# One core, two transformer blocks: the first eight experts named early, a second selection spread between dot products, and the last output slab by token tiles

## The chip, the cores and the metric

The kernel runs on one core of a Trainium2 chip. Its time is the device time of one execution in microseconds (us); three timed runs of the kernel before gave 3590.76, 3593.22 and 3593.61, so the median is 3593.22 us. A core has TensorE (PE) for matrix products, VectorE (DVE), ScalarE (ACT), GpSimd (POOL), and SyncE (SP), which here only issues transfers. The sixteen DMA engines are shared by the queues of SP, ACT and POOL. Each engine works through its own list of instructions in order and waits on semaphores.

## What is computed

256 tokens of width 2048 pass through two blocks. The end of the first one is a layer of 16384 single-neuron experts, and the end of the second one is an output product with a layer norm:

```python
def peer(h, ...):                       # h: 256 x 2048, 8 heads
    q = (h @ w_query)                   # per head two halves of 128
    s1, s2 = q[..., 0] @ sub_keys_1.T, q[..., 1] @ sub_keys_2.T   # 128 scores each
    v1, i1 = top_k(s1, 16);  v2, i2 = top_k(s2, 16)
    cand = v1[:, None] + v2[None, :]    # 256 pairs
    top_s, pos = top_k(cand, 16)        # 16 pairs, position in the 16 x 16 square
    idx  = i1[pos // 16] * 128 + i2[pos % 16]
    gate = softmax(top_s)
    act  = (expert_down[idx] * h).sum(-1)            # 16 dots of 2048
    return sum_k gate * gelu(act) * expert_up[idx]   # 16 scaled rows of 2048
...
y = (o * silu(z)) @ w_out               # end of the second block, 2048 x 2048
x = layer_norm(alpha * x + y, g, b)     # the kernel's output
```

All of it is float32. The kernel makes a float32 product from three: an operand is split into a rounded high part and the rest (the low part), and high*high, low*high and high*low are added.

## The kernel before, in words

Weights come in parts of 256 rows by 512 columns (512 KB). SP loads a part into one of four ring places, ACT rounds it into the high part (`split_hi`, in the second block `mla_hi`), POOL or DVE subtracts it from the original to get the low part (`split_lo`, `mla_lo`), and PE multiplies: 12 products of 128x512 a part, six for each token tile of 128. Eight parts are a slab of 512 output columns. SP loads the next part into a ring place when its low part has been made (`lo_made`), and ACT overwrites a high part when PE has used it (`parts_used`).

**The expert layer** works in row heads: a row head is one token tile of one of the eight heads, so there are 16, in four rounds of four. Row head 0 is tile 0 of head 0, row head 1 is tile 0 of head 1, row heads 2 and 3 are the same two heads for tile 1.

1. `first_queries_pe`, `first_queries_act` and `first_queries_dve` make the queries of round 0 (the slab W_PQ). PE first does the eight parts for tile 0. ACT then scales them (`take_tile_rows`), PE turns them (`turn_tile_queries`), ACT copies them (`take_tile_queries`), PE scores them against the keys (`score_tile_keys`) and ACT copies the scores. Meanwhile PE does the eight parts for tile 1; the turn stands behind the first of these and the scoring behind the second. DVE scales the normed input for both tiles (`h2`).
2. DVE selects in `choose(chosen, step)`, steps 0 to 5: the best 16 of two lists (0 and 1), the best 16 of 256 pairs (2 and 3), the decoding of these into expert numbers (4 and 5). Before the change it does all of `choose(0)` (row head 0), which releases POOL by `experts_ready`, then all of `choose(1)`, then the 16 dots of row head 0.
3. POOL gathers one row of 2048 floats for each of 128 tokens with an indirect DMA (1 MB a row). The order is fixed by `row_table`: the 16 down rows of row head 0, then in turn an up row of head h and a down row of head h+1. There are eight places, four for down and four for up rows; row head 0's down rows use both. `load_row` waits until the row that had the place is used, and POOL issues in order. The first row also waits until PE has used all parts of W_PQ for both tiles, since held parts lie in the up places.
4. DVE multiplies a down row with `h2` and sums it (`dot_row`). After 16, ACT does the gelu (`gelu_head`), DVE multiplies by the gates (`weigh_head`), ACT spreads each weight on a diagonal (`spread_weight`), and PE adds the up rows with these (`sum_row`).
5. The weights of round 1's queries (slab W_PQ+1) are split meanwhile. POOL makes the low parts of parts 0 to 3 before it starts gathering. DVE makes those of parts 4 to 7 behind the dots 1, 3, 5 and 7 of row head 0. PE then makes the queries, ACT takes them and then rounds the first four parts of slab W_PQ+2. SP can load each of these four only when one of the low parts 4 to 7 is there. All of this stands in ACT's list ahead of the gelu of row head 0 (the end of `first_queries_act`, L1144 to L1154; the gelu is at L2127).

**The end of the kernel** is the product `mo` in four slabs of eight parts, part by part and in each part both tiles (`mla_part`). Behind the last part DVE adds the slab to the residual (L1755), takes the moments, ACT the root, DVE normalises four quarters of both tiles (`ln_last`), and SP stores a quarter of both tiles when it is done.

Of the kernel before, what the change touches and what calls it, by code (L numbers as in the profile page):

```python
# [7 lines left out]
F32 = mybir.dt.float32  # L8
# [3 lines left out]
ALU = mybir.AluOpType  # L12
# [10 lines left out]
PK = 2  # L23
# [253 lines left out]
M_FIRST = PARTS * W_CQ  # L277

# [79 lines left out]
def program(nc, I, out, table, stream, wide, narrow, latent, early, matrices):  # L358
    ctx = ExitStack()
    with ctx:  # L360
# [98 lines left out]
        gain_all = down_rows[:, ROWS - 1]  # L459
# [76 lines left out]
        ringf = ring.rearrange("p s k n -> p s (k n)")  # L536

# [46 lines left out]
        normal_high, tile_made = sem("normal_high"), sem("tile_made")  # L584

# [472 lines left out]
        def first_queries_pe(pe):  # L1058
# [62 lines left out]
        def first_queries_act(act):  # L1121
# [32 lines left out]
        def first_queries_dve(dve):  # L1154
# [19 lines left out]
            for t in range(NT):  # L1174
                m = nc.vector.scalar_tensor_tensor(out=h2[:, t], in0=X[:, t], scalar=full_inv[:, t:t + 1], in1=gain_all,
                                                   op0=ALU.mult, op1=ALU.mult)
            m.then_inc(h2_ready, 1)
# [212 lines left out]
        def mla_fill(sp):  # L1390

            at = {"uq": 0, "ckv": 0, "": 0}
            for n, (kind, _, _) in enumerate(M_ORDER):
                sp.wait_ge(lo_made, M_FIRST + n - RING + 1)
# [4 lines left out]
        def mla_hi(act, n):  # L1399

            act.wait_ge(part_in[n % RING], 16 * ((M_FIRST + n) // RING + 1))
            act.wait_ge(parts_used, M_FIRST + n - RING + 1)
            at = slice(0, mla_width(n))
            nc.scalar.activation(w_hif[:, n % RING, at], ringf[:, n % RING, at], ACT.Copy).then_inc(hi_made, 1)  # L1404
# [32 lines left out]
        def mla_part(pe, n):  # L1437
# [31 lines left out]
            by_tile = [(t, k) for t in range(NT) for k in range(PK)]  # L1469
            by_row = [(t, k) for k in range(PK) for t in range(NT)]  # L1470
            for step, (t, k) in enumerate(by_tile if (kind, i) == ("mo", 3) and last else by_row):
# [6 lines left out]
                    if (kind, i) == ("mo", 3) and last and step == PK - 1:  # L1478
                        mm.then_inc(tile_made, 1)
# [227 lines left out]
        def mla_dve(dve, n):  # L1707
# [40 lines left out]
            if kind == "mo" and u == PARTS - 1:  # L1748
                for t in range(NT):
                    if i == 3 and t == 0:  # L1750
                        dve.wait_ge(tile_made, 2)
                    else:
                        mla_made(dve, kind, i, u)
# [3 lines left out]
                    if i == 3:  # L1757
                        slab_moments(dve, i, [t])
                if i < 3:
                    slab_moments(dve, i)  # L1760
# [151 lines left out]
        def ln_last(dve):  # L1912

            dve.wait_ge(ln_in, 64)
            for q in range(4):
                at = slice(q * NC, (q + 1) * NC)
                for t in range(NT):
                    nc.vector.scalar_tensor_tensor(out=X[:, t, at], in0=X[:, t, at], scalar=ln_moments[:, t, 0:1],
                                                   in1=last_gain[:, at], op0=ALU.subtract, op1=ALU.mult)
                dve.drain()  # L1920
                for t in range(NT):
                    last = nc.vector.scalar_tensor_tensor(out=X[:, t, at], in0=X[:, t, at],
                                                          scalar=full_inv[:, t:t + 1], in1=last_shift[:, at],
                                                          op0=ALU.mult, op1=ALU.add)
                last.then_inc(ln_done, 1)
# [1280 lines left out]
```

## Time and profile before

| | |
|---|---|
| median of three runs | 3593.22 us |
| the profiled execution's own time | 3590.01 us |
| its span | 3588.2 us |
| PE busy | 3246.1 us (90%) |
| DVE, ACT, POOL busy | 1746.6, 1332.4, 2196.0 us |
| moved by DMA | 936.79 MB, mean 261 GB/s |
| of these gathered by POOL | 538.74 MB |
| mean granted clock of TensorE | 0.984 |

The span goes from the first to the last instruction of one traced execution. The page of the profile splits it into 40 slices of 89.7 us; the expert layer's gathers lie in slices 10 to 24, and in slices 11 to 23 (897 to 2063 us) the 16 DMA engines are busy nine tenths or more and move 417 to 421 GB/s. Outside of slices 10 to 24 the rate is 139 to 230 GB/s and PE is busy nine tenths of nearly every slice. A full clock is 1.0, which is 2.4 GHz, and 0.5 is 1.2 GHz.

### The profile page before, as it was taken

How to read it: one execution, taken by the hardware profiler on the slowest of the kernel's cores; microseconds unless marked ns; L12 is line 12 of the kernel's file. 1: busy time of each engine (PE TensorE's matmuls, PEld its weight loads, DVE VectorE, ACT ScalarE, POOL GpSimd, SP SyncE). 2: the span in 40 equal slices, each digit the busy share in tenths (PEclk: the TensorE clock that was granted, in tenths of full speed). 3: DMA queues.
4: the chain of work that ended last, by engine and by line, in shares of the span. 5: the costliest groups of instructions: out<-in, count | busy, mean ns of one | idle time of the engine just before them, and what ended most of it. 6: DMA issues, size and time to landing. Idle time of an engine off the chain costs nothing.

```text
span 3588.2 us, 38812 instructions
## 1 busy us (share of the span) xinstructions
PE 3246.1 (90%) x13642; PEld 2304.9 (64%) x13642; DVE 1746.6 (49%) x2565; ACT 1332.4 (37%) x2037; POOL 2196.0 (61%) x1221
## 2 busy tenths in 40 slices
PE   9999999996787788777777789999999999999998
PEld 7888878884343334322322348888888888878886
DVE  8998264238566457544744452222222223435443
ACT  6776575442111011000100014444444444445553
POOL 2021767876545545454555438888788778878666
PEclk9999999998999999999999999999999999999999
DMA  7455545659999999999999985555555545555444
GB/s 230 139 150 139 169 148 161 225 186 378 419 419 420 421 418 420 421 419 421 421 417 421 419 339 187 176 172 174 166 175 174 171 166 176 174 178 181 147 143 163
DMA packets 232701, 936.79 MB, mean 261 GB/s; under 512 B 28112, under 2 KB 31184, under 8 KB 165968
## 3 DMA queue, kind: packets, MB, share of 16 engines
q0 software_dynamic: 76288, 538.74, 36.3%
q1 hardware_dynamic: 152784, 391.96, 33.6%
q10 hardware_dynamic: 3456, 3.77, 0.3%
q8 instruction: 110, 1.80, 0.2%
q14 instruction: 63, 0.52, 0.0%
HBM read 927.04 MB, written 2.10 MB: 259 GB/s over the span
## 4 chain that ended last, share of the span: by engine, by line
PE 64%; DMA 25%; DVE 5%; POOL 2%; issue 1%; DVEq 1%; ACT 1%; ACTq 0%; SPq 0%
PE products L671 41%; DMA arena<-peer_up_in,arena 20%; PE products L2120 7%; PE products L1476 7%; DMA arena<-peer_down_in,arena 4%; POOL arena L2066 2%; DVE arena L2075 1%; PE products L1207 1%; PE products L2682 1%; PE products L1313 1%; PE products L2644 1%; PE products L1230 1%; POOL weights_low L1410 1%; DVE weights_low L630 0%; PE products L1450 0%
## 5 line engine op out<-in xcount | busy, mean ns | idle before, releaser
L630 POOL TENSOR_TENSOR weights_low<-arena,weights_high 128x1024 fp32r<-128x1024 f32 x484 | 1187.9, 2462 | 367.8 <-ACT weights_high L618 323.9
L2120 PE MATMUL products<-arena 128*128 128x512 f32 x1984 | 940.5, 621 | 288.4 <-DMA arena<-peer_up_in,arena 230.1
L618 ACT ACTIVATE weights_high<-arena 128x1024 fp32r<-128x1024 f32 x604 | 637.8, 1059 | 972.0 <-PE products L671 952.5
L671 PE MATMUL products<-weights_high,input_high 128*128 128x512 f32 x2416 | 984.7, 408 | 14.2 <-DVE weights_low L630 12.6
L671 PE MATMUL products<-weights_low,input_high 128*128 128x512 f32 x2416 | 945.7, 391 | 0.0
L671 PE MATMUL products<-weights_high,input_low 128*128 128x512 f32 x2416 | 943.3, 390 | 0.0
L2120 PEld LDWEIGHTS products<-arena 128*128 128x128 f32 x1984 | 372.0, 196 | 839.0 <-issue 427.2
L2075 DVE SCALAR_TENSOR_TENSOR arena<-arena 128x2048 f32<-128x2048 f32 x256 | 586.0, 2292 | 524.5 <-DMA arena<-peer_down_in,arena 524.0
L2066 POOL DMA_INDIRECT arena<-peer_up_in,arena x256 | 385.8, 1507 | 528.0 <-PE products L2120 504.3
L671 PEld LDWEIGHTS products<-weights_high,input_high 128*128 128x128 f32 x2416 | 455.4, 189 | 110.0 <-DVE weights_low L630 14.3
L671 PEld LDWEIGHTS products<-weights_low,input_high 128*128 128x128 f32 x2416 | 454.2, 188 | 98.8
L671 PEld LDWEIGHTS products<-weights_high,input_low 128*128 128x128 f32 x2416 | 455.6, 189 | 92.3 <-issue 4.5
L2066 POOL DMA_INDIRECT arena<-peer_down_in,arena x256 | 282.5, 1104 | 113.3 <-issue 75.3
L1410 POOL TENSOR_TENSOR weights_low<-arena,weights_high 128x1024 fp32r<-128x1024 f32 (+2 forms) x120 | 268.8, 2248 | 96.2 <-ACT weights_high L1404 93.4
L2136 ACT ACTIVATE arena<-arena 128x128 f32<-128x128 f32 x248 | 91.5, 397 | 561.5 <-PE products L2120 541.6
L1404 ACT ACTIVATE weights_high<-arena 128x1024 fp32r<-128x1024 f32 (+2 forms) x116 | 113.3, 977 | 143.9 <-PE products L1476 133.1
L1476 PE MATMUL products<-weights_high,arena_rounded 128*128 128x512 f32 (+1 forms) x512 | 155.4, 384 | 0.0
L630 DVE TENSOR_TENSOR weights_low<-arena,weights_high 128x1024 fp32r<-128x1024 f32 x120 | 146.2, 1222 | 9.7 <-ACT weights_high L618 8.8
L1247 DVE TENSOR_TENSOR arena<-products,arena 128x128 f32<-128x128 f32 x96 | 29.8, 352 | 239.9 <-PE products L1207 239.9
L2389 POOL COPY arena<-arena 128x252 f32<-128x252 f32 x16 | 19.8, 1266 | 206.7 <-DVE arena L2484 206.7
L1782 DVE TENSOR_TENSOR arena<-products,arena 128x1024 f32<-128x1024 f32 (+3 forms) x41 | 34.3, 838 | 188.1 <-PE products L671 185.1
L2127 ACT ACTIVATE arena<-arena 128x16 f32<-128x16 f32 x16 | 3.5, 217 | 286.8 <-DVE arena L2080 286.8
(352 smaller groups left out, 3038.0 us busy)
## 6 DMA issues: line engine op xcount, KB each, us to landing
arena<-dsa_in SPq DMA_DIRECT2D x320, 512.0 KB, 3.5
arena<-w_in_in SPq DMA_DIRECT2D x128, 512.0 KB, 3.8
arena<-mla_wide_in SPq DMA_DIRECT2D x88, 512.0 KB, 3.5
arena<-w_attn_o_in SPq DMA_DIRECT2D x32, 512.0 KB, 4.3
arena<-w_out_in SPq DMA_DIRECT2D x32, 512.0 KB, 4.7
arena<-peer_w_query_in SPq DMA_DIRECT2D x32, 512.0 KB, 7.8
arena<-dsa_w_out_in SPq DMA_DIRECT2D x32, 512.0 KB, 3.7
arena<-glu_w_b_in SPq DMA_DIRECT2D x16, 512.0 KB, 3.8
```

The costliest lines, as they stand in the source:

```text
L618: nc.scalar.activation(w_hi[:, u % RING, :, at], ring[:, u % RING, :, at], ACT.Copy).then_inc(hi_made, 1)
L630: ops.tensor_tensor(w_lo[:, u % RING, :, at], ring[:, u % RING, :, at], w_hi[:, u % RING, :, at].bitcast(F32), op=ALU.subtract).then_inc(l ...
L671: mm = nc.tensor.matmul(PS[:, bank(b) + t, 0:width], x[:, x0 + n, at], y, start=n == 0 and m == 0, stop=n == len(parts) * PK - 1 and m == 2)
L1207: mm = nc.tensor.matmul(PS[:, D_SCORE_BANK, at:at + seen], QKD[:, buf, k, 0, t * P:(t + 1) * P], QKD[:, buf, k, 1, 0:seen], start=True, st ...
L1230: nc.tensor.matmul(PS[:, O_BANK, col:col + SEQ], VD[:, buf, g, 0], PTD[:, s % 2, 0:2 * P], start=g == 0, stop=False)
L1404: nc.scalar.activation(w_hif[:, n % RING, at], ringf[:, n % RING, at], ACT.Copy).then_inc(hi_made, 1)
L1410: nc.gpsimd.tensor_tensor(w_lof[:, n % RING, at], ringf[:, n % RING, at], w_hif[:, n % RING, at].bitcast(F32), op=ALU.subtract).then_inc(l ...
L1476: mm = nc.tensor.matmul(banks[:, t, 0:width], x[:, x0 + PK * u + k, q], y, start=u == 0 and k == 0 and m == 0, stop=last and k == PK - 1 a ...
L2066: pool.indirect_dma_start(row_place(kind, h, n), None, I["peer_" + kind][0], bass.IndirectOffsetOnAxis(ap=experts[:, r, t, p, n:n + 1], ax ...
L2075: nc.vector.scalar_tensor_tensor(out=row, in0=row, scalar=1.0, in1=h2[:, t], op0=ALU.mult, op1=ALU.mult, accum_out=acts[:, h % 2, n:n + 1])\
L2120: mm = nc.tensor.matmul(PS[:, SUM_BANKS[q]], diag[:, d % ROWS], row[:, q * NC:(q + 1) * NC], start=h % 2 == 0 and n == 0, stop=bool(last))
L2136: nc.scalar.activation(diag[:, d % ROWS], ident, ACT.Copy, scale=weights[:, h % 2, n:n + 1]).then_inc(diag_ready, 1)
```

## The change

Three things change. First, in `choose(0)` the first eight experts are decoded directly behind the first eight maxima (`halve_best`, `name_experts`) and POOL is released for eight rows; the other eight follow. For this PE turns and scores tile 0 before it starts on tile 1, only one tile of `h2` is scaled ahead of the choice (the other behind the first dot of row head 1; the gain's vector waits in its place and is loaded later), and POOL makes three low parts ahead of the gathers and the fourth behind the fourth row. Second, the six steps of `choose(1)` stand behind the dots 0 to 5 of row head 0, and the low parts 4 to 7 of W_PQ+1 behind the dots 9, 11, 13 and 15. Third, the last slab of `mo` is done by tiles: its last four parts are rounded into the space of the normed input, so that all eight parts are there; PE does tile 0 with all of them, then tile 1; DVE finishes tile 0 while PE does tile 1; eight stores replace four. DVE makes the last five low parts in place of POOL.

```diff
@@ first_queries_pe
             mm.then_inc(queries_made, 1)
+            turn_tile_queries(pe, 0)
+            score_tile_keys(pe, 0)
             for u in range(PARTS):
                 query_part(pe, 0, u, [1])
-                if u == 0:
-                    turn_tile_queries(pe, 0)
-                if u == 1:
-                    score_tile_keys(pe, 0)
@@ first_queries_act
             take_tile_queries(act, 0)
-            next_hi(act, 0)
             take_tile_scores(act, 0)
             load_keys(act, 1)
-            for u in range(1, RING):
+            for u in range(RING):
                 next_hi(act, u)
@@ choose, with halve_best and name_experts cut out of its steps 3 to 5
+            best = slice(TOPK // 2, TOPK) if chosen == 0 else slice(0, TOPK)
+            if chosen == 0 and step == 2:
+                dve.drain()
+                for s in range(2):
+                    halve_best(dve, chosen, s, slice(0, TOPK // 2))
+                name_experts(dve, chosen, slice(0, TOPK // 2))
             if step in (4, 5):
...
+                halve_best(dve, chosen, step - 4, best)
             if step == 5:
...
+                name_experts(dve, chosen, best)
@@ POOL
-            split_lo(pool, nc.gpsimd, W_PQ + 1, 0, range(RING))
+            split_lo(pool, nc.gpsimd, W_PQ + 1, 0, range(RING - 1))
             pool.wait_ge(h2_ready, 1)
             pool.wait_ge(parts_used, PARTS * (W_PQ + 1))
             for kind, h, n in ROW_ORDER:
-                if kind == "down" and n == 0 and (h < 3 or h % 4 == 0):
-                    pool.wait_ge(experts_ready, h // 4 + 3 if h >= 4 else h + 1)
+                if kind == "down" and (h == 0 and n == TOPK // 2 or n == 0 and (h < 3 or h % 4 == 0)):
+                    pool.wait_ge(experts_ready, experts_of(h, n))
                 load_row(pool, kind, h, n)
+                if (kind, h, n) == ("down", 0, RING - 1):
+                    split_lo(pool, nc.gpsimd, W_PQ + 1, 0, [RING - 1])
...
-            for n in range(len(M_ORDER)):
+            for n in range(POOL_LAST):
                 mla_lo(pool, n)
@@ DVE
-            for chosen in range(2):
-                for step in range(CHOICES - 1):
-                    choose(dve, chosen, step)
+            for step in range(CHOICES - 1):
+                choose(dve, 0, step)
             for n in range(TOPK):
                 dot_row(dve, 0, n)
-                if n % 2 and n // 2 < RING:
+                if n < CHOICES - 1:
+                    choose(dve, 1, n)
+                if n % 2 and n // 2 >= RING:
                     dve.wait_ge(hi_made, PARTS * (W_PQ + 2))
-                    split_lo(dve, nc.vector, W_PQ + 1, 0, [RING + n // 2])
+                    split_lo(dve, nc.vector, W_PQ + 1, 0, [n // 2])
...
+                    if (h, n) == (0, 0):
+                        scale_rows(dve, 1)
                     rows_dve(dve, h, n)
...
-            for n in range(len(M_ORDER) + 1):
+            for n in range(M_LAST):
                 mla_dve(dve, n)
-            row_moments(dve)
-            ln_inverse(dve, 1)
-            ln_last(dve)
+            for n in range(POOL_LAST, M_LAST + PARTS):
+                last_lo(dve, n)
+            mla_dve(dve, M_LAST)
+            for t in range(NT):
+                last_rows(dve, t)
@@ the last slab: mla_hi rounds parts 4 to 7 without waiting for parts_used, into the space of XH and XL
+        def last_lo(dve, n):
+            dve.wait_ge(hi_made, M_FIRST + n + 1)
+            nc.vector.tensor_tensor(mla_half(1, n), ringf[:, n % RING], mla_half(0, n).bitcast(F32), op=ALU.subtract)\
+                .then_inc(last_low, 1)
+        def last_slab(pe):
+            for t in range(NT):
+                for u in range(PARTS):
...
+                    for k in range(PK):
+                        for m, (x, y) in enumerate(((YHR, hi), (YLR, hi), (YHR, lo))):
+                            mm = nc.tensor.matmul(banks[:, t], x[:, PK * u + k, q], y, ...)
+                mm.then_inc(last_made, 1)
+        def last_rows(dve, t):
+            dve.wait_ge(last_made, t + 1)
+            # residual, moments, root on ACT, four quarters of one tile, each released to SP
@@ SP
+            for t in range(NT):
+                for q in range(4):
+                    sp.wait_ge(ln_done, PARTS + 4 * t + q + 1)
+                    sp.dma_start(out[0, t * P:(t + 1) * P, at], X[:, t, at]).then_inc(out_done, 16)
```

## Rows read from the trace of the kernel before

**Rows 1.** Page, part 4: the chain that ended last, by line.

```profile
PE products L671 41%; DMA arena<-peer_up_in,arena 20%; PE products L2120 7%; PE products L1476 7%; DMA arena<-peer_down_in,arena 4%; POOL arena L2066 2%; DVE arena L2075 1%; PE products L1207 1%; PE products L2682 1%; PE products L1313 1%; PE products L2644 1%; PE products L1230 1%; POOL weights_low L1410 1%; DVE weights_low L630 0%; PE products L1450 0%
```

**Rows 2.** Windows: length, busy PE, PEld, DVE, ACT, POOL (instructions); clock, DMA, GB/s.

```profile
872.00:876.00 4.00, 4.00 (x6) 1.40 (x6) 2.22 (x2) 0.32 (x2) 3.39 (x3) 0.50 1.02 424
1100.00:1500.00 400.00, 317.57 (x740) 137.83 (x739) 228.38 (x306) 44.56 (x103) 196.46 (x155) 0.97 1.01 420
```

**Rows 3.** Chain of waits in order of time, its last long piece: start, length, what.

```profile
3516.31 53.08 PE products L1476 x234
```

**Rows 4.** Timeline of PE, 795 to 900 us: start, length, instruction [idle before <-releaser].

```profile
801.04 1.05 PE L1089 MATMUL products<-arena 128*128 128x128 f32 x8
...
871.59 16.56 PE L2120 MATMUL products<-arena 128*128 128x512 f32 x32 [14.39 <-ACT arena L2136]
```

**Rows 5.** Timeline of DVE, 802 to 832 us.

```profile
802.76 0.49 DVE L1955 MAX8 arena<-arena 128x8 f32<-128x128 f32 x2 [1.82 <-ACT arena L1118]
...
809.67 2.02 DVE L1999 TENSOR_SCALAR arena<-arena 128x16 uint32<-128x16 uint32 x1
...
815.50 0.18 DVE L2019 CAST arena<-arena 128x16 uint32<-128x16 f32 x1
...
826.40 2.29 DVE L2075 SCALAR_TENSOR_TENSOR arena<-arena 128x2048 f32<-128x2048 f32 x1
...
830.83 1.22 DVE L630 TENSOR_TENSOR weights_low<-arena,weights_high 128x1024 fp32r<-128x1024 f32 x1
```

**Rows 6.** Timeline of ACT, 798 to 870 us.

```profile
798.11 0.69 ACT L1106 ACTIVATE arena<-products,arena 128x512 f32<-128x512 f32 x1 [3.13 <-PE products L671]
...
810.34 0.69 ACT L1106 ACTIVATE arena<-products,arena 128x512 f32<-128x512 f32 x1 [4.25 <-PE products L671]
...
860.85 1.06 ACT L618 ACTIVATE weights_high<-arena 128x1024 fp32r<-128x1024 f32 x1 [2.58 <-DMA arena<-peer_w_query_in]
861.93 1.28 ACT L2127 ACT_TABLE_LOAD   x1
869.27 0.22 ACT L2127 ACTIVATE arena<-arena 128x16 f32<-128x16 f32 x1 [6.05 <-DVE arena L2080]
```

**Rows 7.** Timeline of POOL, 804 to 879 us.

```profile
804.27 7.38 POOL L630 TENSOR_TENSOR weights_low<-arena,weights_high 128x1024 fp32r<-128x1024 f32 x3 [0.34 <-ACT weights_high L1097]
816.60 1.05 POOL L2066 DMA_INDIRECT arena<-peer_down_in,arena  x1 [4.94 <-DVE arena L2019]
...
860.66 0.95 POOL L2066 DMA_INDIRECT arena<-peer_up_in,arena  x1 [8.91 <-DVE arena L2075]
...
878.12 1.89 POOL L2066 DMA_INDIRECT arena<-peer_up_in,arena  x1 [1.84 <-PE products L2120]
```

**Rows 8.** Line L2066, gathers issued at 821.73, 860.66 and 878.12 us, from issue.

```profile
DMA to landing us min/median/max: 11.5/11.5/11.5
...
DMA to landing us min/median/max: 8.8/8.8/8.8
...
DMA to landing us min/median/max: 12.2/12.2/12.2
```

**Rows 9.** Tile peer_w_query_in: weight parts issued 826 to 900 us, beside gathered rows.

```profile
DMA to landing us min/median/max: 10.3/10.9/11.9
```

**Rows 10.** Tile peer_w_query_in: weight parts issued 803 to 812 us, without gathers.

```profile
DMA to landing us min/median/max: 3.4/3.6/3.7
```

**Rows 11.** Timeline of DVE, 3571 us to the end.

```profile
3571.16 0.67 DVE L1755 SCALAR_TENSOR_TENSOR arena<-arena,products 128x512 f32<-128x512 f32 x1
...
3573.68 1.41 DVE L1918 SCALAR_TENSOR_TENSOR arena<-arena 128x512 f32<-128x512 f32 x2
...
3583.61 1.41 DVE L1922 SCALAR_TENSOR_TENSOR arena<-arena 128x512 f32<-128x512 f32 x2
```

**Rows 12.** Timeline of ACT at the start of the last slab; of SP at the end.

```profile
3549.07 1.06 ACT L1404 ACTIVATE weights_high<-arena 128x1024 fp32r<-128x1024 f32 x1 [1.66 <-PE products L1476]
...
3576.61 8.81 SPq L2897 DMA_DIRECT2D out<-arena  x4
```

More of the change, by code:

```diff
@@ L277 @@
 M_FIRST = PARTS * W_CQ
+M_LAST = len(M_ORDER) - PARTS
+POOL_LAST = M_LAST + RING - 1
 def mla_turns():
@@ L536, in program @@
         ringf = ring.rearrange("p s k n -> p s (k n)")
+        beside = [x[:].rearrange("p k t -> p (k t)").rearrange("p (s n) -> p s n", s=RING) for x in (XH, XL)]
         part_in = [sem(f"part_in{s}") for s in range(RING)]
@@ L1173, in first_queries_dve, with scale_rows @@
             dve.wait_ge(gain_in, 16)
[L1174 to L1177, printed above, removed]
+            scale_rows(dve, 0)
+        def scale_rows(dve, t):
+            nc.vector.scalar_tensor_tensor(out=h2[:, t], in0=X[:, t], scalar=full_inv[:, t:t + 1], in1=gain_all,
+                                           op0=ALU.mult, op1=ALU.mult).then_inc(h2_ready, 1)
         def hi_part(act, n):
@@ new lines, in mla_half @@
+        def mla_half(a, n):
+            return beside[a][:, n - M_LAST - RING] if n >= M_LAST + RING else (w_hif, w_lof)[a][:, n % RING]
+        def last_lo(dve, n):
[3 more added lines that the diff above has]
+        def last_slab(pe):
+            banks = mla_bank("mo", 3)
+            mla_emptied(pe, "mo", 3, 0)
+            for t in range(NT):
+                q = slice(t * P, (t + 1) * P)
+                for u in range(PARTS):
+                    n = M_LAST + u
+                    if t == 0:
+                        pe.wait_ge(lhs_lo, L_MO + u + 1)
+                        if n < POOL_LAST:
+                            pe.wait_ge(lo_made, M_FIRST + n + 1)
+                        else:
+                            pe.wait_ge(last_low, n - POOL_LAST + 1)
+                    for k in range(PK):
+                        hi, lo = (mla_half(a, n)[:, k * NC:(k + 1) * NC] for a in range(2))
+                        for m, (x, y) in enumerate(((YHR, hi), (YLR, hi), (YHR, lo))):
+                            mm = nc.tensor.matmul(banks[:, t], x[:, PK * u + k, q], y, start=u == 0 and k == 0 and m == 0,
+                                                  stop=u == PARTS - 1 and k == PK - 1 and m == 2)
+                mm.then_inc(last_made, 1)
@@ L1406, in mla_lo, with last_roots @@
+        def last_roots(act, t):
+            act.wait_ge(summed, 2 + t)
+            nc.scalar.activation(full_root[:, t:t + 1], ln_moments[:, t, 1:2], ACT.Sqrt, bias=eps_ln).then_inc(roots, 1)
         def mla_lo(pool, n):
@@ L1468, in mla_part @@
             last = u == (UP_PARTS if kind in ("uq", "ukv") else PARTS) - 1
-            by_tile = [(t, k) for t in range(NT) for k in range(PK)]
-            by_row = [(t, k) for k in range(PK) for t in range(NT)]
-            for step, (t, k) in enumerate(by_tile if (kind, i) == ("mo", 3) and last else by_row):
+            for k in range(PK):
+                for t in range(NT):
                     at = slice(k * width, (k + 1) * width)
@@ L1910, in finish_rows @@
                                                op0=ALU.mult, op1=op)
[L1912 to L1925, printed above, removed]
         def ln_load(sp, n):
@@ L2893, in _ @@
             ln_load(sp, 1)
[L2894 to L2898 removed]
+            for t in range(NT):
+                for q in range(4):
+                    at = slice(q * NC, (q + 1) * NC)
+                    sp.wait_ge(ln_done, PARTS + 4 * t + q + 1)
+                    sp.dma_start(out[0, t * P:(t + 1) * P, at], X[:, t, at]).then_inc(out_done, 16)
+            sp.wait_ge(out_done, 16 * 4 * NT)
         @block.gpsimd
@@ L3023, in _ @@
                 mla_act(act, n)
-            ln_act(act, 1)
+            for t in range(NT):
+                last_roots(act, t)
         @block.vector
@@ L3155, in _ @@
                 normal_turn_pe(pe, u)
-            for n in range(len(M_ORDER)):
+            for n in range(M_LAST):
                 mla_part(pe, n)
```

100 lines of the change are left out of this document (61 added, 39 removed).

## The prediction

> **What bounds the kernel.** I read the chain of waits first: 41% of the span is weight products, 20% and 4% are gathers of up and down rows on the way [rows 1]. The windows say which of the two rules where: between 1100 and 1500 us the DMA engines are never free (share 1.01, 420 GB/s) while PE is busy 318 of 400 us [rows 2]. So the expert layer is a stream of 1.05 MB rows at 2.5 us each; it ends earlier only if it starts earlier and never runs dry, and a hole in it is never made up. Behind it PE rules to the end: the last piece of the chain is 234 products in 53.08 us, 0.227 us each [rows 3], and then, from 3569.4, 18.8 us of the span remain for the layer norm and the stores. The change touches the start of the stream and these last microseconds. I work out each in the clock of the profiled execution.
>
> **A. The first gather.** POOL issues the first row at 816.60, having waited for DVE's choice, which ended at 815.68 [rows 5, 7]. Now:
>
> - *DVE starts earlier.* ACT has the rows of tile 0 at 798.80 [rows 6] and PE scores at 801.04 [rows 4]. In between stand 12 products of tile 1, 2.7 us at 0.227, some of which only fill the wait for ACT. Without them the gain lies between 0 and 2.2 us; a turn, a copy and their hand-offs (1.4 us, an estimate) remain, so I take 0.85: the choice starts at 801.9 and not at 802.76 [rows 5].
> - *It is shorter to the first release.* From 802.76 to 809.67 are the maxima; the second eight of the pairs (1.1 us) move behind, so decoding starts at 801.9+5.8 = 807.7. Decoding 16 took 809.67 to 815.68 = 6.0; in it the first instruction took 2.02 where a cast of the same size takes 0.18 [rows 5], a gap of 1.85 that is no work. The rest is 4.15; six wide operations of about 0.43 at half width cost between 0.21 and 0.43, I take 0.28, and the gate's argument (0.15) moves out: 3.1. Released at 810.8 without the gap, 812.7 with it.
> - *But PE is later.* POOL also waits until tile 1's products are done; ACT saw that at 810.34 [rows 6]. They now start behind the scores, at 801.0, and 48 x 0.227 is 10.9: 812.2 with the drain.
> - *POOL's splits don't bind.* Three at 2.46 (7.38 for three [rows 7]) instead of four end at 811.1.
>
> With the hand-off of 0.3 to 0.9 (815.68 to 816.60) the first row is issued between 812.5 and 813.7. I take 813.4, **3.2 us earlier**.
>
> **B. The 16 dots.** The row issued at 821.73, the fifth, lands 11.5 us later [rows 8]; four rows back at 2.5 the first landed at 823.2, 6.6 after its issue. So now at 820.0. DVE has the other eight experts by 812.7+1.3+3.1 = 817.1 and sits idle for 3 us, since its next instruction is the first dot. Before, it did the second choice (815.68 to 826.40, 10.7 us [rows 5]) in just this time; now that stands between the dots. 16 dots at 2.21 (two and no gap from 826.40 to 830.83 [rows 5]) are 35.4, the choice 10.7 and its six starts 0.6, three splits of 1.13 ahead of the last dot 3.4: the dots end at 870.1. Before they ended at 869.2, when the gelu came [rows 6]. **The early start is used up on DVE.** The 13th dot, which frees the place of the first up row, ends at 862.3; POOL issues that row at 862.7 and not at 860.66 [rows 7].
>
> For the stream this is a first hole. From 817.5 the 16 rows (40 us) and two weight parts (0.52 MB, 1.25 us each) keep DMA busy to 860; the up row issued at 862.7 lands 6.6 later, 869.3, where it landed at 860.66+8.8 = 869.5 before [rows 7, 8]. The lead of 3.2 is gone, and two weight parts are still to come.
>
> **C. The gelu of row head 0.** This is the edit with a hidden cost. ACT's list has the four parts of slab W_PQ+2 ahead of the gelu, and SP loads the last of them when DVE has split part 7 of W_PQ+1. Before, that split followed the eighth dot (848.7); the part landed at 860.85, ACT had the gelu's table at 863.2, and then waited 6.05 us for the dots [rows 6]. Now the split follows the 16th dot: 870.2+1.13 = 871.3, issue 871.5. Beside gathers such a part lands 10.3 to 11.9 us after issue, median 10.9 [rows 9]: 882.4. Then 1.06 to round, 1.28 for the table, 0.25 for the gelu [rows 6]: 885.0. Behind the gelu wait DVE (its product with the gates, then all dots of row head 1), then ACT's diagonals, PE's sums, and through them POOL: 0.7 us later, at 885.7, PE starts the first up row, on the low clock as before (0.50 [rows 2]), where POOL's next up row followed 871.59 by 6.5 us [rows 4, 7]. It is issued at 892.2, not 878.12.
>
> The eight rows in flight cover part of that: from 866 they and two weight parts take 22.5 us, to 888.5. The row issued at 892.2 finds the queue empty and lands at 898.8; before it landed at 878.12+12.2 = 890.3 [rows 7, 8]. **The stream is 8.5 us late**, and as it is bound by DMA to its end it stays so. The ends: a landing after 10.3 or 11.9, a first up row at the full clock (3.4 us, estimated as the rest of the 16.56 us for four [rows 4] over three) and the dots' end between 868 and 871.5 give +3 to +11.
>
> A rule of the Trainium skill would make this smaller. The row says 10.9 us beside gathers and 3.6 without [rows 9, 10]. "DMA: Bandwidth & Descriptors", section on queues, rings and completion order, says that each DMA engine takes turns between the queues, a whole packet at a time. A part would then wait for about one packet of a row, and land some 6 us after issue (an estimate by that page); the hole would be near 4 us and the sum 3591. The trace does not agree, and I go by it.
>
> **D. Small moves.** Scaling the second tile of `h2` (2.3 us, the size of a dot [rows 5]) leaves DVE where it waited 1.82 us anyway [rows 5] and comes back among row head 1's dots, where DMA paces: 0, at most 2.3. The gain's load on ACT's queue moves by 12 parts, under products that have four parts of lead: 0 to 0.5. POOL's fourth split (2.46) falls behind the fourth row, with 10 us of rows queued: 0.
>
> **E. The last slab.** PE's products are the same 96 for both tiles. Tile 0 needs all eight parts in 48 x 0.227 = 10.9 us, so one every 1.36 us instead of 2.72. ACT's rounding of these waited for PE, not for data (1.66 us idle a part [rows 12]); now the last four wait for nothing of PE, and DVE, idle here, splits at 1.2 us where POOL takes 2.4. Part 3 is rounded at 3549.1 to 3550.1 [rows 12] and the other four follow at 1.06 or with their loads, 3.6 us after issue [rows 10]: the last low part is there at about 3557.5, and PE wants it at 3549.0+7x1.36 = 3558.5. No stall; PE ends at 3570.7 as before. Tile 0 is finished under tile 1.
>
> What is left behind PE is one tile. Before: residual of the second tile at 3571.16, normalising from 3573.68 to 3585.02 [rows 11], last store issued at 3585.4 and landed by 3588.2. After: the residual at 3570.8, 2.4 us to the normalising (one tile's statistics), four quarters of two operations at 0.70 plus a drain of 0.08 for each quarter, minus overlap, 5.7 us: 3578.9. The store is then as long: **6.1 us earlier** (5 to 6.5).
>
> **The sum.** 3590.0 + 8.5 - 6.1 = 3592.4 for the profiled execution. The runs' median lies 3.2 us above it (3593.2), so I forecast 3595.6.
>
> **Rivals.**
>
> 1. *The stream never runs dry.* If the eight rows in flight cover the late gelu, and the dots keep their lead, the change gives what it says: 3593.2-3.2-6.1 = 3583.9. For it: the cover is 20 us and the gelu only 15 late. Against: the 13th dot and the choice between the dots, which are sums of plain durations. Chance 0.16.
> 2. *The last part lands early.* If at 871.5 the queue is thin, the part lands as without gathers, 3.6 later [rows 10], the up row is issued at 884.9 before the queue is empty (888.5), and only two weight parts that fall behind instead of ahead remain, less 1 us of earlier rows: +1.5. 3593.2+1.5-6.1 = 3588.6. Against: all four parts in rows 9. Chance 0.12. The skill's rule named in C lies between this and the forecast.
> 3. *Slower: tile 0 of the last slab starves.* If low parts keep coming every 2.72 us, as ACT and POOL gave them before, the eighth is there 5 us late (five parts after the third, at 3563.5), PE waits, and the tail gains 1.1 instead of 6.1: 3593.2+8.5-1.1 = 3600.6. It decides from the point where the last low part is later than 3558.5. For it: SP loads a part only when the one four before it is split. Against: nothing in that loop is longer than 3.6+1.06+1.2. Chance 0.12.
>
> **Chances.** Forecast 0.60 (its own range 3589 to 3599). This kernel's runs can tell about 0.2%, 7 us, from no change, so below 3586 is faster and above 3600.4 slower. Faster: rival 1 and an edge of the forecast, 0.18. Slower: rival 3 and an edge with the larger hole, 0.15. Same: 0.67. The range 3584 to 3602 takes in the forecast's ends, rival 2, most of rival 3 and about half of rival 1.
>
> **What would show it.** After the change: the first gather near 813 and the last dot of row head 0 near 870; ACT waiting on a weight part around 882 just ahead of the gelu's table; DMA below 400 GB/s around 861 to 866 and 889 to 895; POOL's fifth up row near 892. At the end one tile's normalising, 5.7 us, behind PE, with no wait of PE inside the last 96 products. A gelu before 876, or dots done before 866, would prove step C or B wrong; a PE gap near 3557 would prove E wrong.

## The result, and the profile after

The kernel before takes 3591.94 us (median of 21 runs, 3590.73 to 3594.03), the changed one 3597.89 us (21 runs, 3595.40 to 3601.14): ratio 1.0015, 95% interval 1.0009 to 1.0021. It is slower by 6 us, less than the 0.2% that the prediction set as the bound of "same". The profiled execution has a span of 3594.0 us. It and the one before reach ACT's scaling of tile 0 at the same time (798.12 and 798.11 us), so that from there their clocks can be compared as they stand.

The start of the stream, POOL's timeline from 804 to 896 us (start, length, instruction [idle before <-releaser]). It answers to [rows 7]:

```profile
804.06 7.45 POOL L634 TENSOR_TENSOR weights_low<-arena,weights_high 128x1024 fp32r<-128x1024 f32 x3 [13.38 <-ACT weights_high L1099]
815.16 1.05 POOL L2131 DMA_INDIRECT arena<-peer_down_in,arena  x1 [3.65 <-DVE arena L2041]
...
820.02 2.42 POOL L634 TENSOR_TENSOR weights_low<-arena,weights_high 128x1024 fp32r<-128x1024 f32 x1
...
864.76 2.75 POOL L2131 DMA_INDIRECT arena<-peer_up_in,arena  x1 [10.58 <-DVE arena L2140]
...
894.71 0.94 POOL L2131 DMA_INDIRECT arena<-peer_up_in,arena  x1 [15.20 <-PE products L2185]
```

The first row is issued 1.4 us earlier, the first up row 4.1 us later, the fifth up row 16.6 us later. What this does to the DMA engines stands in the windows (length, busy PE, PEld, DVE, ACT, POOL; clock, DMA, GB/s). Before the change, from 850 to 910 us:

```profile
850.00:910.00 60.00, 37.77 (x96) 17.19 (x95) 44.60 (x84) 12.96 (x23) 35.01 (x24) 0.83 1.02 417
```

After it, where the same 60 us have a share of 0.84 and 329 GB/s, in pieces:

```profile
860.00:868.00 8.00, 4.22 (x18) 2.85 (x17) 8.00 (x9) 0.00 (x0) 2.94 (x2) 1.00 0.30 105
868.00:892.00 24.00, 14.64 (x53) 9.82 (x54) 11.50 (x17) 9.16 (x16) 9.69 (x7) 0.82 1.00 396
892.00:898.00 6.00, 6.00 (x13) 2.58 (x12) 5.84 (x23) 0.49 (x2) 1.89 (x2) 0.85 0.39 111
904.00:1000.00 96.00, 75.67 (x179) 32.74 (x178) 56.66 (x76) 12.72 (x27) 53.14 (x39) 0.98 1.01 419
```

There are two holes, stretches in which the DMA engines lack work: 8 x (1 - 0.30/1.02) = 5.6 us and 6 x (1 - 0.39/1.02) = 3.7 us without transfers; behind them the stream is full again and gives nothing back. In the first, DVE is busy 8.00 of 8.00 us: the dots hold the places. The second is made by ACT and by what feeds it. ACT's timeline, 878 to 888 us, answers to the last lines of [rows 6]:

```profile
878.16 1.27 ACT L2368 ACTIVATE arena<-products,arena 128x512 f32<-128x512 f32 x2 [37.96 <-PE products L675]
...
881.61 3.90 ACT L622 ACTIVATE weights_high<-arena 128x1024 fp32r<-128x1024 f32 x4 [0.23 <-issue]
885.53 1.28 ACT L2192 ACT_TABLE_LOAD   x1
886.82 0.22 ACT L2192 ACTIVATE arena<-arena 128x16 f32<-128x16 f32 x1
```

ACT stood 37.96 us before the next round's query rows, rounded four parts without a pause and reached the gelu of row head 0 at 886.82; before it was 869.27. DVE had its sixteen dots long since:

```profile
802.03 0.49 DVE L1996 MAX8 arena<-arena 128x8 f32<-128x128 f32 x2 [3.34 <-ACT arena L1120]
...
809.31 2.23 DVE L2024 CAST arena<-arena 128x16 f32<-128x16 uint32 x1
...
814.07 0.17 DVE L2041 CAST arena<-arena 128x8 uint32<-128x8 f32 x1
...
820.96 3.64 DVE L2140 SCALAR_TENSOR_TENSOR arena<-arena 128x2048 f32<-128x2048 f32 x1 [1.99 <-DMA arena<-peer_down_in,arena]
...
872.46 1.23 DVE L634 TENSOR_TENSOR weights_low<-arena,weights_high 128x1024 fp32r<-128x1024 f32 x1
...
887.08 0.18 DVE L2150 TENSOR_TENSOR arena<-arena 128x16 f32<-128x16 f32 x1 [11.86 <-ACT arena L2192]
```

That is DVE's timeline, answering to [rows 5]. The choice starts at 802.03, as forecast; the last split, of part 7, ends the dots' stretch, and DVE idles 11.86 us for the gelu. The last of the weight parts that hang on that split, issued at 873.85 beside gathers, in the view of its tile:

```profile
DMA to landing us min/median/max: 10.5/10.5/10.5
```

as in [rows 9]. At the end, the timelines of ACT, PE, DVE and SP (these answer to [rows 11] and [rows 12]):

```profile
3559.70 1.06 ACT L1411 ACTIVATE weights_high<-arena 128x1024 fp32r<-128x1024 f32 x1 [1.66 <-PE products L1540]
...
3567.94 1.06 ACT L1411 ACTIVATE input_high<-arena 128x1024 fp32r<-128x1024 f32 x1 [2.86 <-DMA arena<-mla_wide_in]
...
3562.42 0.43 SPq L1970 DMA_DIRECT2D arena<-ln_g_in  x1
3562.89 0.43 SPq L1970 DMA_DIRECT2D arena<-ln_b_in  x1
...
3570.41 0.70 PE L1440 MATMUL products<-input_high,arena_rounded 128*128 128x512 f32 x2 [1.28 <-DVE input_low L1420]
...
3582.97 0.69 DVE L1448 SCALAR_TENSOR_TENSOR arena<-arena,products 128x512 f32<-128x512 f32 x1 [1.77 <-PE products L1440]
...
3576.76 15.01 SPq L2963 DMA_DIRECT2D out<-arena  x8
```

ACT's rounding of part 3 of the last slab, its last that waits for PE, is a good mark: from it to the end there were 3588.2 - 3549.07 = 39.13 us [rows 12], now 3594.0 - 3559.70 = 34.30. The tail gains 4.83 us, with a wait of PE of 1.28 us in it.

### The profile page after: what moved, and what is told of

The parts are those of the page before. It is cut to its first block, busy times and chain, and to the rows that moved or that the text cites. A ratio compares the mean times of both kernels' runs of the same rounds, so it can differ in the third digit from the quotient of the medians.

```text
span 3594.0 us, 38848 instructions
## 1 busy us (share of the span) xinstructions
PE 3244.2 (90%) x13642; PEld 2303.4 (64%) x13642; DVE 1759.0 (49%) x2582; ACT 1334.4 (37%) x2038; POOL 2188.9 (61%) x1216
## 4 chain that ended last, share of the span: by engine, by line
PE 64%; DMA 25%; DVE 6%; POOL 2%; issue 1%; DVEq 1%; ACT 1%; ACTq 0%; SPq 0%; POOLq 0%
PE products L675 41%; DMA arena<-peer_up_in,arena 21%; PE products L2185 8%; PE products L1540 6%; DMA arena<-peer_down_in,arena 3%; DVE arena L2140 2%; POOL arena L2131 1%; PE products L1210 1%; PE products L2747 1%; PE products L1316 1%; PE products L2709 1%; PE products L1233 1%; POOL weights_low L1475 1%; DVE weights_low L634 1%; PE products L1222 0%
## 5 line engine op out<-in xcount | busy, mean ns | idle before, releaser
L1475 POOL TENSOR_TENSOR weights_low<-arena,weights_high 128x1024 fp32r<-128x1024 f32 (+2 forms) x115 | 257.4, 2248 | 93.8 <-ACT weights_high L1411 90.7
L1540 PE MATMUL products<-weights_high,arena_rounded 128*128 128x512 f32 (+1 forms) x448 | 135.7, 384 | 0.0
```

The source lines that it names most:

```text
L1475: nc.gpsimd.tensor_tensor(w_lof[:, n % RING, at], ringf[:, n % RING, at], w_hif[:, n % RING, at].bitcast(F32), op=ALU.subtract).then_inc(l ...
L1540: mm = nc.tensor.matmul(banks[:, t, 0:width], x[:, x0 + PK * u + k, q], y, start=u == 0 and k == 0 and m == 0, stop=last and k == PK - 1 a ...
```

## The experiments

Theory at this point: the second choice between the dots makes the first hole (DVE holds the places longer), the late splits make the second (gelu late), the tail gains 4.8 us, and DMA gives no hole back. For each kernel I read one row, the window from 850 to 910 us, and took 60 x (1 - share/1.02) as the time without transfers.

**One part alone.** `e1_tail_only` is the kernel before with the third part of the change; `e2_rows_only` the changed kernel without it.

> The kernel before with the last slab by token tiles and nothing else of the change. Theory: in the changed kernel's trace the stretch from the first part of that slab to the end of the span is 4.8 us shorter (34.3 us from ScalarE's rounding of its fourth part to the end, against 39.1 before), and nothing earlier is touched, so this kernel should be 4.8 us faster than before: a ratio of 0.9987. Rival: the tail's gain is only apparent (it hides work that the later stream had already made late), then the ratio is 1.0000.

3587.66 us, ratio 0.9986 (0.9977 to 0.9995); from the mark to the end 34.08 us. As expected.

> The changed kernel with the last slab as before. Theory: the two holes in the DMA stream near 862 to 868 and 892 to 898 us stay, everything behind them is 10.6 us late to the end, ratio 1.0030. Rival: part of the shift is caused by something else in the tail's edit, then under 1.0020.

3602.12 us, ratio 1.0027 (1.0016 to 1.0038), share 0.86 from 850 to 910. That is as expected, though the lower end of the interval leaves room for the rival's 1.0020. The two halves have opposite signs, -5.3 and +9.1 us, and the change is their sum within 2.2 us.

**The place of the splits.** `e3_splits_mid`, from the changed kernel:

```diff
-                if n % 2 and n // 2 >= RING:
+                if n in (5, 6, 7, 8):
                     dve.wait_ge(hi_made, PARTS * (W_PQ + 2))
-                    split_lo(dve, nc.vector, W_PQ + 1, 0, [n // 2])
+                    split_lo(dve, nc.vector, W_PQ + 1, 0, [n - 1])
```

> The changed kernel, but VectorE's splits of parts 4 to 7 of the next pair's query weights stand behind dots 5, 6, 7 and 8 in place of 9, 11, 13 and 15; the second choice stays between the dots. Theory that the late splits make the first gelu late: the splits end near 848 us, the last weight part is issued some 25 us earlier (before 850), gelu waits for the last dot alone (some 873), the second hole of the DMA stream is gone, the head's fifth up row lands at 892 to 894 us (900.3 in the changed kernel), and the time falls by 6 to 8 us against it, to a ratio of 0.9995 to 1.0000 against before. Rival, that the choice between the dots is the whole cause: the dots end no earlier, the fifth up row still lands near 900, ratio 1.0015 as the changed kernel.

3592.93 us, ratio 1.0001 (0.9992 to 1.0011). The gelu comes at 874.77, right behind the last dot, and the second hole is gone; the windows of this kernel:

```profile
860.00:874.00 14.00, 6.06 (x37) 4.78 (x35) 14.00 (x13) 7.66 (x11) 5.20 (x3) 0.92 0.67 241
890.00:900.00 10.00, 6.22 (x14) 2.34 (x13) 7.27 (x18) 0.80 (x2) 7.35 (x6) 0.96 1.01 418
```

But the fifth up row lands at 898.06, not at 892 to 894: four splits in place of two now stand ahead of the thirteenth dot, which ends at 867.91 (864.48 in the changed kernel; 1.1 of these 3.4 us are this execution's own, whose ACT scales tile 0 at 799.26), so one hole of 14 x (1 - 0.67/1.02) = 4.8 us remains. Moving the splits gives back 5.3 us of time without transfers (10.6 to 5.3), 4.0 us of the gathers' length (table below) and 6.0 us of time, each kernel against its own runs of before: about 4 to 6 us, where I expected 6 to 8. Both rival causes are real, one for each hole.

`e5_late_splits_in_before` does the reverse in the kernel before: only the splits are moved, to dots 9, 11, 13 and 15.

> The kernel before, with one edit: VectorE's splits of parts 4 to 7 of the next pair's query weights behind dots 9, 11, 13 and 15 in place of 1, 3, 5 and 7. Theory that the late splits by themselves make the first gelu late: the last weight part is issued some 870 us in place of 849 and lands near 880 beside row gathers, the first gelu starts near 880 to 885 (869 before), the fifth up row lands at 893 to 897 (890.3 before), ratio 1.0008 to 1.0018. Rival, that they are harmless without the choice between the dots: gelu near 870, ratio 0.9995 to 1.0002, since four splits fewer stand ahead of the first up row.

3596.35 us, ratio 1.0010 (1.0001 to 1.0019), as expected. The gelu is at 881.37 with the same roundings just ahead of it, and a hole appears where the kernel before had none (windows; 6 x (1 - 0.66/1.02) = 2.1 us):

```profile
860.00:870.00 10.00, 4.95 (x17) 3.73 (x18) 8.89 (x15) 0.00 (x0) 8.78 (x5) 0.91 1.01 391
886.00:892.00 6.00, 6.00 (x15) 2.66 (x14) 5.83 (x25) 0.80 (x2) 2.67 (x3) 1.00 0.66 234
```

So the late splits do this by themselves, and the first hole does not come from them.

**ACT's order.** `e6_gelu_first`, from the changed kernel:

```diff
+            gelu_head(act, 0)
             take_query_rows(act, 1)
...
-            split_hi(act, W_PQ + 2, 0, range(RING))
...
+                    if (h, n) == (0, 3):
+                        split_hi(act, W_PQ + 2, 0, range(RING))
```

> The changed kernel with ScalarE's gelu of the first head put ahead of the rounding of the next pair's query rows, and the four roundings of the pair after it put behind the head's fourth weighing; VectorE's order is the changed kernel's. Theory that the second hole comes from ScalarE's order alone: gelu starts within 2 us of the last dot (872 to 874 in place of 886.8), no hole at 892 to 898, the fifth up row lands near 892 to 894, the first hole at 862 to 868 stays, time 5 to 6 us under the changed kernel, ratio 0.9998 to 1.0003. Rival, that the second hole would come anyway (VectorE or the gathers' landing sets it): ratio 1.0012 or more.

3593.95 us, ratio 1.0003 (0.9994 to 1.0012), as expected. Gelu and windows of this kernel:

```profile
873.35 0.22 ACT L2192 ACTIVATE arena<-arena 128x16 f32<-128x16 f32 x1 [30.98 <-DVE arena L2145]
```

```profile
860.00:870.00 10.00, 6.42 (x25) 4.63 (x24) 10.00 (x9) 0.00 (x0) 4.06 (x2) 0.95 0.43 151
890.00:900.00 10.00, 10.00 (x24) 4.26 (x23) 6.62 (x16) 1.21 (x3) 7.00 (x6) 1.00 1.02 414
```

With DVE's order unchanged the second hole is gone and the first is as large as in the changed kernel (a share of 0.43 from 860 to 870 us, 0.41 there). The fifth up row lands at 898.17, later than I expected, but out of a full queue, so it costs nothing. This settles the second hole: it is four roundings and the query rows standing ahead of a gelu on ACT, when the splits that feed them are late. (`e3_splits_mid` has the same order on ACT, early splits and no second hole.)

**The choice in one piece.** `e4_choice_first` is the changed kernel with the two edits to DVE's order undone (the splits are back behind dots 1, 3, 5 and 7):

```diff
-            for step in range(CHOICES - 1):
-                choose(dve, 0, step)
+            for chosen in range(2):
+                for step in range(CHOICES - 1):
+                    choose(dve, chosen, step)
```

> The changed kernel with both choices ahead of the dots and the splits behind dots 1, 3, 5 and 7 as before; the early decoding of eight experts and the tail by tiles stay. Theory: no hole in the DMA stream near 862 or 892 us, the fifth up row lands as before (890) or up to 1.5 us earlier, and only the tail's 4.8 us is gained: ratio 0.9983 to 0.9988. Rival, that the order of the second choice doesn't matter (the shift comes from the early gathers): ratio 1.0010 or more.

3589.02 us, ratio 0.9990 (0.9981 to 0.9999). The hole near 892 is gone, and the one near 862 is down to 10 x (1 - 0.87/1.02) = 1.5 us, not to nothing as I expected:

```profile
860.00:870.00 10.00, 2.05 (x16) 1.86 (x16) 10.00 (x11) 5.37 (x6) 4.63 (x2) 0.80 0.87 321
890.00:900.00 10.00, 7.44 (x17) 2.88 (x16) 7.33 (x18) 0.81 (x2) 5.60 (x5) 1.00 1.01 419
```

The fifth up row lands at 894.60, 4.3 us later than before; 1.4 of them are this execution's own (its ACT scales tile 0 at 799.49). The theory holds for both holes, the size of the gain only nearly: the early decoding, which stays in, has a price (below). The profiled execution also lost 2 us in the tail, told under the unexpected findings.

**The stall in the tail.** `e7_tail_ln_early` is the tail alone, with the loads of the last gain and shift issued one slab earlier:

```diff
+                if n == M_LAST - PARTS:
+                    sp.wait_ge(parts_used, M_FIRST + M_PART["ukv", MLA_PAIRS - 1, UP_PARTS - 1] + 1)
+                    ln_load(sp, 1)
...
-            sp.wait_ge(parts_used, M_FIRST + M_PART["ukv", MLA_PAIRS - 1, UP_PARTS - 1] + 1)
-            ln_load(sp, 1)
```

> The kernel before with the last slab by token tiles, and the last gain and shift rows loaded one slab earlier than before. Theory that the TensorE stall of 1.28 us in the changed kernel's last slab comes from its last weight part landing 5.9 us after issue beside those loads: it lands in about 3.5 us, the stall is gone, 6.1 us faster than before, ratio 0.9983. Rival, that the part is late for another reason (its issue waits for VectorE's split): the stall stays, ratio 0.9987 as with the tail alone.

3587.96 us, ratio 0.9984 (0.9974 to 0.9993). ACT's timeline of this kernel:

```profile
3554.35 1.06 ACT L1415 ACTIVATE weights_high<-arena 128x1024 fp32r<-128x1024 f32 x1 [1.66 <-PE products L1544]
...
3561.15 1.06 ACT L1415 ACTIVATE input_high<-arena 128x1024 fp32r<-128x1024 f32 x1 [1.35 <-DMA arena<-mla_wide_in]
```

The last part lands 4.43 us after issue instead of 5.87, PE shows no wait in the last slab, and from the mark to the end there are 3587.2 - 3554.35 = 32.85 us: the tail gains 6.28 us. By timing alone it cannot be told from `e1_tail_only`; the stall and its cause are shown by the traces.

**What is the early decoding worth?** `e8_choice_first_ln_early` adds to that kernel only the early decoding (with PE's, POOL's and the scaling's moves that go with it).

> The changed kernel with both choices ahead of the dots, the splits as before, and the last gain and shift rows loaded one slab earlier. It differs from the kernel with the tail alone and early loads by the early decoding of eight experts only. Theory that the early decoding is worth nothing, because the DMA stream runs dry for the same time whichever row comes first: ratio 0.9983, equal to that kernel. Rival, that it moves the whole stream of rows earlier by the 1.4 us of its first gather: ratio 0.9979.

3588.34 us, ratio 0.9986 (0.9977 to 0.9995). Its interval holds both forecasts, 0.9983 and 0.9979. The trace is clearer: the first gather is 1.8 us earlier than in `e7_tail_ln_early` (816.37 against 818.16), the first dot 3.1 us later (831.05 against 827.97), and 1.2 us of hole remain (share 1.00). My last pair put both into an order in which DVE's splits (behind the last four dots) and ACT's roundings are out of the way, the gelu as in `e6_gelu_first`: `e9_late_splits_gelu_first` with the early decoding, `e10_same_order_no_early_decode` without. The splits in `e9_late_splits_gelu_first`, from `e8_choice_first_ln_early`:

```diff
-                if n % 2 and n // 2 < RING:
+                if n >= TOPK - RING:
                     dve.wait_ge(hi_made, PARTS * (W_PQ + 2))
-                    split_lo(dve, nc.vector, W_PQ + 1, 0, [RING + n // 2])
+                    split_lo(dve, nc.vector, W_PQ + 1, 0, [n - PARTS])
```

> The changed kernel with both choices ahead of the dots, VectorE's four splits behind the last four dots, ScalarE's first gelu ahead of the next pair's query rows with the roundings behind the fourth weighing, and the last gain and shift rows loaded one slab earlier. Theory that the early decoding paid nothing only because VectorE's dots (with four splits of 1.14 us ahead of the thirteenth) gave back the buffers no earlier: the thirteenth dot ends near 858 to 860 us, the stream runs dry for under 1 us near 866 (2.6 us with the splits early), the first gelu stays at 870 to 872, and the whole row stream is 2 to 3 us earlier than in the kernel that differs in these orders alone; ratio 0.9976 to 0.9981. Rival, that the early start is lost for another reason, or that the late query parts of the next pair make a new hole: ratio 0.9984 or more.

> As the other kernel of this call, but without the early decoding: all sixteen experts of a head are decoded after both choices, as in the kernel before. Theory: the DMA stream had no hole to close in that order, and it starts 1 to 2 us later, so the new order is worth nothing here: ratio 0.9983 to 0.9986, as with the tail and the early gain and shift alone. Rival, that the new order by itself speeds the stream: ratio under 0.9980 and no difference from the other kernel.

`e9_late_splits_gelu_first`: 3588.75 us, ratio 0.9987 (0.9978 to 0.9996). `e10_same_order_no_early_decode`: 3586.78 us, ratio 0.9981 (0.9972 to 0.9990), the lowest median of all. The theory as I wrote it falls: without any split ahead of the thirteenth dot the early start still pays nothing. First gather, first dot and windows with it:

```profile
816.80 1.05 POOL L2134 DMA_INDIRECT arena<-peer_down_in,arena  x1 [3.65 <-DVE arena L2044]
...
831.50 2.29 DVE L2143 SCALAR_TENSOR_TENSOR arena<-arena 128x2048 f32<-128x2048 f32 x1
```

```profile
860.00:866.00 6.00, 4.47 (x11) 3.50 (x12) 6.00 (x7) 0.00 (x0) 4.78 (x3) 0.50 0.61 216
```

and without it, first dot and windows:

```profile
827.82 2.29 DVE L2120 SCALAR_TENSOR_TENSOR arena<-arena 128x2048 f32<-128x2048 f32 x1
```

```profile
860.00:866.00 6.00, 6.00 (x25) 4.85 (x24) 6.00 (x7) 0.00 (x0) 5.39 (x3) 0.88 1.01 411
```

The first gather is at 816.80 against 818.01, but the first dot at 831.50 against 827.82 and the end of the thirteenth at 860.33 against 857.17: decoding in two halves puts 138 instructions in place of 115 between 802 us and the first dot. From the choice's own start (803.71 and 804.17) to the first dot that is 27.8 us in place of 23.6, and some 1.3 us of the difference are casts and shifts that take longer than their work (last section). The stream pays 6 x (1 - 0.61/1.02) = 2.4 us of hole for 1.2 us of earlier start. That the one kernel is truly slower than the other their overlapping intervals don't show, nor whether the new order by itself is better than `e7_tail_ln_early`.

All of it in one table. "Gathers" is the time from the first to the last gather's issue (1303.7 before); single executions differ by up to 1.7 us ahead of the stream (ACT's scaling of tile 0 stands between 798.11 and 799.79), so it is compared within each trace. "Tail" is from the mark to the end.

| kernel | DMA share 850-910 | without transfers | gathers | tail | time - before |
|---|---|---|---|---|---|
| before | 1.02 | 0 | 1303.7 | 39.1 | 0 |
| changed | 0.84 | 10.6 | 1315.9 | 34.3 | +6.0 |
| rows only | 0.86 | 9.4 | 1315.9 | 38.8 | +9.1 |
| gelu first | 0.92 | 5.9 | 1312.4 | 34.3 | +0.7 |
| splits in the middle | 0.93 | 5.3 | 1311.9 | 34.7 | -0.1 |
| late splits in before | 0.98 | 2.4 | 1308.4 | 39.1 | +3.1 |
| late splits, gelu first | 0.98 | 2.4 | 1308.1 | 32.8 | -4.8 |
| choice first | 0.99 | 1.8 | 1307.5 | 36.5 | -4.0 |
| choice first, loads early | 1.00 | 1.2 | 1307.8 | 33.0 | -4.9 |
| tail, loads early | 1.02 | 0 | 1305.5 | 32.9 | -5.3 |
| same order, no early decoding | 1.02 | 0 | 1305.1 | 32.8 | -6.7 |
| tail only | 1.02 | 0 | 1305.1 | 34.1 | -5.3 |

The gathers' length is 1305 plus the time without transfers, within 1.6 us. The time without transfers less the tail's gain (39.1 less the tail) gives the last column within 1 us everywhere but in "choice first", whose profiled execution had the long tail. The last column is a difference of medians, whose intervals are some 3 us to either side, so an agreement to 1 us is closer than the runs can vouch for.

## Why the prediction was right, step by step

The forecast was 3595.6 us, measured 3597.89. The path held: an early start that DVE uses up, a first hole, a late gelu, a second hole, and a tail that gains less than the holes cost. Four terms were off, and two signs came out against the prediction: ACT didn't wait on a weight part ahead of the gelu (C), and PE did wait in the last slab (E). As a change it is +2.4 us forecast against +6.0 measured. The time came out closer than that because the three runs that the forecast started from had a median 1.3 us above that of the 21. That is luck, and a range of 18 us is wide for a change of 6.

- **A, the first gather.** 813.4 forecast, 815.16 measured: earlier by 1.4 us, not 3.2. DVE's start, PE's part and POOL's splits came as forecast (802.03, 812.33 and 811.5). The step that failed is "released at 810.8 without the gap, 812.7 with it": I counted one gap of 1.85 us, and DVE lost time at three instructions, casts and shifts of 0.2 us that took 1.46, 0.78 and 2.23 us; the release came at 814.07+0.17.
- **B, the dots.** Forecast to end at 870.1, measured 872.26; 13th dot 862.3 against 864.48. Of the 2.2 us, 0.96 came from the start (820.96 against 820.0) and 1.2 from the length, 51.3 us where 50.1 were forecast; the first dot alone, which took 3.64 us, is 1.36 over the others. The first hole is shown by its window, and `e4_choice_first` and `e5_late_splits_in_before` tie it to the choice between the dots. B put the extra work of the early decoding into DVE's idle time ahead of the first dot, and there it fits (1.99 us of idle time are left). Where the choice stands in one piece it doesn't: by the traces of the last pair it then costs more than the early start wins, on the very engine on which the lead was lost.
- **C, the gelu.** Its end was forecast at 885.0 and came at 887.04; fifth up row issued at 892.2 against 894.71. The part landed 10.47 us after issue (10.9 forecast), as in [rows 9]; in the first hole, where rows are few, the three parts ahead of it took 5.22, 3.51 and 5.42 us, so the delay goes with the rows. By the rule of the Trainium skill that the prediction weighed ("DMA: Bandwidth & Descriptors", section on queues, rings and completion order) it would have been some 6 us, an estimate by that page; the trace does not agree here either. The wait that C named is not the one that the trace shows. ACT waited 37.96 us for PE's queries, until 878.16, and then worked without a pause for a part; the fourth began at 884.47, as the third ended, and the part had landed at 884.32. PE's queries hang on the last split too (its last 12 products began at 873.74), so the late splits are the cause by either way, but that the two ways took the same time is luck. An earlier landing alone would have gained next to nothing, so rival 2 would have failed even if its condition had held. `e6_gelu_first` shows that the order on ACT decides.
- **D, small moves.** The second tile of `h2` was scaled at 889.38 for 2.35 us, between the first two dots of row head 1. It cost the stream nothing there, since POOL's next row waited for PE until 894.71.
- **The hole.** 8.5 us late forecast; 10.6 us without transfers in the trace, 9.1 us in `e2_rows_only`'s time. The range of +3 to +11 held it.
- **E, the tail.** 6.1 us forecast, 4.83 measured (5.3 in `e1_tail_only`'s time). The failed sentence is "the other four follow at 1.06 or with their loads, 3.6 us after issue": the last part took 5.87 because SP issued the loads of gain and shift 0.37 and 0.84 us behind it, and PE waited 1.28 us. That is rival 3 on a small scale, and the sign that the prediction named against E, a PE gap near 3557. By its working PE wants the eighth part at 3558.5; that is 3569.1 in the changed execution, by the mark, and PE stood from 3569.13 to 3570.41. `e7_tail_ln_early` takes these loads away and the tail gains 6.28.

Rival 1 is refuted by the two holes, and its price, 9.3 us under before, appears in no kernel: the best that decodes early is 4.9 us under (`e8_choice_first_ln_early`), no better than the tail alone.

## What to carry to other kernels

When a resource is full for most of a kernel, look at its start: the gain is the earlier start minus every hole, so price first what the change adds to the engine that gives buffers back, here DVE with 23 instructions and 10.7 us of choice against 1.4 us won. When work is moved later on one engine, follow its results through the in-order queues of the others: four splits on DVE went through SP's loads, PE and ACT's list to a gelu that had nothing to do with them, and moving that gelu ahead gave some 5 us back. And a load for later use, issued right behind the last load that the end waits for, makes that one late: 5.87 us in place of 4.43.

## What I had not expected of the hardware

- A dot on DVE of 128x2048 floats took 3.64 us while POOL made a split beside it (820.02 to 822.44), and 2.28 to 2.31 otherwise. The kernels that share this order show the same (3.59 to 3.83 us). What of it is POOL's doing was not tried.
- Some small DVE instructions took 0.6 to 2 us more where they are first executed in the choice than at their next execution: 2.24 us for a cast of 128x16 in `e9_late_splits_gelu_first`, 0.21 us at its next execution 6.7 us later. The kernel before has the same at other lines (2.02 us in [rows 5]). Why was not tried.
- A short wait may cost twice. In `e4_choice_first` PE waited 1.84 us in the last slab, and the granted clock of the next 5 us was 0.66 (15 products, 24 in the 5 us behind): from 3566.0 to 3569.2 it was 0.50, which is 1.2 GHz. The tail became 36.45 us. After waits of 1.09 to 1.74 us in four other kernels the clock stayed at 2.4 GHz. It is one execution, and that the wait caused the fall is not shown. The windows of that kernel:

```profile
3560.00:3565.00 5.00, 3.17 (x14) 2.30 (x14) 1.84 (x3) 2.42 (x3) 0.00 (x0) 1.00 0.96 390
3565.00:3570.00 5.00, 4.99 (x15) 3.96 (x16) 4.31 (x9) 0.42 (x2) 0.00 (x0) 0.66 0.10 39
3570.00:3575.00 5.00, 5.00 (x24) 4.12 (x23) 4.74 (x7) 0.00 (x0) 0.00 (x0) 1.00 0.28 105
```
